# A two-block transformer in fp32: the order of the first projection after a stage boundary, and the place of one statistic on VectorE

## The reference

```python
def rms_norm(x, w):
    return x * rsqrt(mean(x * x, -1) + EPS) * w

def swiglu(h, w_in, w_out):                 # width 2816
    gate, up = split(h @ w_in, 2)
    return (silu(gate) * up) @ w_out

def memory_cross_attention(h, mem_n, w_q, w_k, w_v, w_o):   # 4 heads of 256
    q, k, v = h @ w_q, mem_n @ w_k, mem_n @ w_v
    return softmax(q @ k.T * 256 ** -0.5) @ v @ w_o

# first block
x = x + 0.5 * swiglu(rms_norm(x, ..), ..)
x = x + hybrid_mixer(rms_norm(x, ..), ..)   # a state-space scan beside differential attention
x = x + memory_cross_attention(rms_norm(x, ..), rms_norm(mem, ..), ..)
x = rms_norm(x + 0.5 * swiglu(rms_norm(x, ..), ..), ..)
# second block, two layers: ffn, mixer (pooling, then sparse attention), cross attention, ffn
for i in range(2):
    x = x + 0.5 * swiglu(..); x = x + mixer_i(..)
    x = x + memory_cross_attention_2(..); x = x + 0.5 * swiglu(..)
return rms_norm(x, final_norm)
```

## Time and profile before

| | |
|---|---|
| Time, median of 3 runs | 1930.49 us (1930.22 to 1930.87) |
| The profiled execution | 1930.22 us, its span 1928.4 us |
| TensorE busy | 1870.8 us, 97% of the span |
| VectorE busy | 1287.6 us, 67% |
| ScalarE busy | 972.1 us, 50% |
| GpSimd busy | 152.1 us, 8% |
| Mean granted TensorE clock | 0.989 of 2.4 GHz |
| DMA engines busy | 324.77 MB moved, mean 168 GB/s |

### The profile page before, as it was taken

The page is one execution under the profiler, slowest core; times in us unless marked ns, Lnnn a source line. Parts: engine busy times, 40 slices in busy tenths (PEclk is TensorE's granted clock), DMA queues, the critical chain, the costliest instruction groups (busy, mean ns, idle before and its releaser), DMA issues.

```text
span 1928.4 us, 32368 instructions
## 1 busy us (share of the span) xinstructions
PE 1870.8 (97%) x13202; PEld 1726.7 (90%) x13202; DVE 1287.6 (67%) x1454; ACT 972.1 (50%) x1322; POOL 152.1 (8%) x169
## 2 busy tenths in 40 slices
PE   6999999999999998999999999999999989999997
PEld 5999999899999997899999999989999859998997
DVE  5676687776566665766785766676668676456665
ACT  5454555575354444444554544454445564454444
POOL 2020100131010003000120100010001001010001
PEclk9999999999999998999999999999999989999998
DMA  6654454334445553554453455545545404435553
GB/s 237 223 197 174 153 186 154 143 123 163 155 150 189 182 188 142 193 187 183 153 197 132 161 189 176 194 175 184 187 176 189 165 23 153 155 125 202 188 182 109
DMA packets 45699, 324.77 MB, mean 168 GB/s; under 512 B 5165, under 2 KB 5301, under 8 KB 6688
## 3 DMA queue, kind: packets, MB, share of 16 engines
q1 hardware_dynamic: 44352, 316.57, 45.4%
q0 software_dynamic: 1248, 6.77, 1.0%
HBM read 322.26 MB, written 1.06 MB: 168 GB/s over the span
## 4 chain that ended last, share of the span: by engine, by line
PE 69%; DVE 7%; POOL 2%; ACT 1%; issue 1%; POOLq 0%; DVEq 0%; ACTq 0%
PE PS L638 20%; PE PS L545 11%; PE PS L546 11%; PE PS L547 11%; PE PS L641 10%; DVE w_lo L1968 3%; DVE xT L1991 2%; DVE x L2035 1%; PE PS L708 1%; PE PS L726 1%; POOL both L459 1%; PE PS L1219 1%; PE PS L1238 1%; PE PS L1258 1%; PE PS L579 0%
## 5 line engine op out<-in xcount | busy, mean ns | idle before, releaser
L1968 DVE TENSOR_TENSOR w_lo<-raw,w_hi 128x2048 fp32r<-128x2048 f32 x298 | 686.5, 2307 | 231.0 <-ACT w_hi L1307 230.7
L638 PE MATMUL PS<-xT,w_hi 128*128 128x512 f32 x2112 | 755.6, 401 | 17.0 <-DVE w_lo L1968 16.2
L1307 ACT ACTIVATE w_hi<-raw 128x2048 fp32r<-128x2048 f32 x299 | 571.1, 1911 | 306.9 <-PE PS L547 295.3
L641 PE MATMUL PS<-xT,w_lo 128*128 128x256 f32 x2112 | 595.0, 282 | 0.0
L638 PEld LDWEIGHTS PS<-xT,w_hi 128*128 128x128 f32 x2112 | 399.8, 189 | 113.6 <-issue 16.2
L641 PEld LDWEIGHTS PS<-xT,w_lo 128*128 128x128 f32 x2112 | 401.7, 190 | 0.2
L545 PE MATMUL PS<-h_hi,w_hi 128*128 128x256 f32 x1280 | 364.3, 285 | 0.0
L546 PE MATMUL PS<-h_lo,w_hi 128*128 128x256 f32 x1280 | 362.1, 283 | 0.0
L547 PE MATMUL PS<-h_hi,w_lo 128*128 128x256 f32 x1280 | 362.0, 283 | 0.0
L545 PEld LDWEIGHTS PS<-h_hi,w_hi 128*128 128x128 f32 x1280 | 245.1, 191 | 4.2 <-DVE h_lo L2115 1.0
L546 PEld LDWEIGHTS PS<-h_lo,w_hi 128*128 128x128 f32 x1280 | 245.2, 192 | 0.2
(11 more groups left out here) (310 smaller groups left out, 2492.4 us busy)
## 6 DMA issues: line engine op xcount, KB each, us to landing
raw<-weights SPq DMA_DIRECT2D x299, 1024.0 KB, 4.8
arena<-mems POOLq DMA_DIRECT2D x5, 1024.0 KB, 6.1
x<-x_in SPq DMA_DIRECT2D x2, 512.0 KB, 4.4
out<-x SPq DMA_DIRECT2D x4, 256.0 KB, 2.6
both<-toep POOLq DMA_DIRECT2D x1, 512.0 KB, 4.1
arena<-toep POOLq DMA_DIRECT2D x1, 512.0 KB, 5.4
con<-consts SPq DMA_DIRECT2D x1, 498.0 KB, 9.5
arena<-dtw SPq DMA_DIRECT2D x1, 256.0 KB, 11.3
```

The source lines that it names most:

```text
L638: pe.matmul(PS[:, bank + part, :], w_hi[:, slot, w:w + P], xT[:, k].rearrange("p a b -> p (a b)"), start=k == 0, stop=False, skip_group_ch ...
L641: last = pe.matmul(PS[:, bank + part, 0:S], w_lo[:, slot, w:w + P], xT_hi[:, k, :], start=False, stop=k == KC - 1, skip_group_check=True)
L1307: act.activation(w_hi[:, slot, :], raw[:, raw_slot, :], ACT.Copy).then_inc(hi_ready, 1)
L1968: dve.tensor_tensor(w_lo[:, slot, :], raw[:, raw_slot, :], w_hi[:, slot, :], ALU.subtract).then_inc(lo_ready, 1)
```

## The change

Two things are reordered; no operation is added or removed.

1. On TensorE, `proj` and `paired` run half 0 with all eight chunks and then half 1, also in the calls with `fresh`. Without `fresh` the order is what it was, and `mid` is still called after the first half. In a fresh call of `proj` the first step of half 1 now carries the flag `start`.
2. On VectorE, the cross stages make the eight low parts of the memory first and the statistic after them.

```diff
@@ proj
-                for part, first in ((0, 0), (0, 4), (1, 0), (1, 4)) if fresh is None else ((0, 0), (1, 0), (0, 4), (1, 4)):
-                    for k in range(first, first + 4):
+                for part in range(2):
+                    for k in range(KC):
                         if fresh is not None and part == 0:
                             pe.wait_ge(split_done, fresh * KC + k + 1)
...
-                        last = mm3(o, a, b, c, d, k == 0 and (part == 0 or fresh is None), k == KC - 1)
-                    if mid is not None and (part, first) == (0, 4):
+                        last = mm3(o, a, b, c, d, k == 0, k == KC - 1)
+                    if mid is not None and part == 0:
                         mid()
@@ cross, VectorE
-                statistic(rcol)
                 for c in range(KC):
                     low_part(c, memx, f"memn{at.mem}", mT_hi, mT_lo, mhi_ready, mlo_ready, at.mem)
+                statistic(rcol)
                 dve.wait_ge(rrow_ready, at.stat)
```

## The result

The changed kernel takes 1942.52 us, the median of 4 executions (1942.16 to 1943.93). The kernel before took 1930.36 beside it (4 executions, 1928.35 to 1930.87). The ratio is 1.0067, with a 95% interval of 1.0053 to 1.0082: slower by 0.67%, 12.2 us. I forecast 1942.0, in a range of 1937.0 to 1945.5. The total came out as forecast; not every term of it did, as will be seen.

The account below looks back on a forecast made before the run. TensorE, busy 1870.8 of 1928.4 us, was taken as the bound, with VectorE's diagonal deciding L579 in most stages. Statistic 6.3, order 2.4 and clock 3.0 gave 11.7 us more: 1942.0 us, range 1937.0 to 1945.5.

Parts of the forecast that it names:

- Part 1: Both cross stages: the statistic behind the memory's eight low parts delays the diagonal and L579 by 3.17 us each, 6.3 us.
- Part 2: First projection after stage boundaries: the new step order costs 2.4 us, mostly at FFN boundaries, after slack before L579.
- lateness d: How much later the first projection after a boundary ends in the new order: 1.06 to 1.42 us.
- the slack before L579 is 0.61: FFN at 560: printed idle 0.46 plus 0.15 absorbs part of 1.11 us lateness, leaving 0.50; two more boundaries repeat this.
- Cross clock: Both cross stages: TensorE stands still 2.57 us, then the clock falls to 1.2 GHz, 1.5 us each, 3.0 us.
- the 2.49 us before: Idle time at 1002.04: the clock fell to 0.50 soon after, and the projection took 7.32 us instead of 5.76.
- The clock did not hold: Rival for the cross stages: no clock fall, or one in two stages; 1939.2 to 1940.7 us, chance 0.29.
- The order in full: Rival at stage boundaries: slack before L579 absorbs no lateness, the new order costs 7.7 us; 1947.5 us, chance 0.12.
- The statistic was not hidden: Rival in the cross stages: sums come later than the low parts, making the move free; 1932.9 us, chance 0.06.
- faster: Rival at 749: TensorE works 1.4 us longer into its wait, keeping the clock up, about 1.5 us won; chance 0.02.

Follow-up runs that it names:

- two shifted kernels: The kernel before with 12 or 24 extra matmuls ahead of the NSA stage's third projection: 1933.09 us (1.0020) and 1934.69 us (1.0023).
- the statistic in the middle: The kernel before with four of the memory's eight low parts ahead of the cross stages' statistic and four behind, old step order: 1933.40 us, 1.0019.
- without the slack: The kernel before with the second weight split moved behind the diagonal: 1922.32 us in the old step order, 1934.41 us with the new order.
- two of the kernels here: Against the kernel before: second split behind the diagonal everywhere, 1922.32 us; the same except in FFN stages, where the row comes two steps later instead, 1926.24 us.

## Why the prediction was right, and where it was not

**Part 1, 6.3 us: right.** 3.16 us in each cross stage of the changed kernel, 3.19 and 3.16 with the statistic moved alone, half of it with half the move, 6.3 in the means (up to 7.2 when a quarter of the clock column is moved). All that was forecast of the place holds: ScalarE's high parts were no obstacle, nothing later in the stage gave the delay back, VectorE's evacuation was 1.21 us idle for ScalarE's row and nobody waited for it.

**Part 2, 2.4 us: right in kind, one term too large.** The first projection's lateness d was 1.07 in cross (forecast 1.06), 1.06 to 1.13 in the FFN (1.11), 1.36 at 1261 and 1.40 at NSA (1.42). It was absorbed as argued. But for each FFN boundary I put 0.50 where the changed kernel shows 0.12, 0.19 and −0.03, and 0.80 where it shows 0.61: 0.9 in place of 2.3. The step that failed is "the slack before L579 is 0.61", which takes the second projection's first half to be 16 uninterrupted matmuls and L579 to cost the same with or without a wait. Two rows show what it left out. The old second projection waited for its own weights; TensorE's weight loads of the kernel before, at 566:

```profile
566.02 0.19 PEld L638 LDWEIGHTS PS<-xT,w_hi 128*128 128x128 f32 x1 [0.17 <-DVE w_lo L1968]
```

and its matmul then, beside the same one after:

```profile
566.03 0.50 PE L638 MATMUL PS<-xT,w_hi 128*128 128x512 f32 x1
```

```profile
569.70 0.50 PE L571 MATMUL PS<-con,both 128*128 128x1 f32 x4
570.06 0.48 PE L638 MATMUL PS<-xT,w_hi 128*128 128x512 f32 x1
...
572.97 0.60 PE L579 MATMUL PS<-both,con 128*128 128x256 f32 x2
573.21 0.58 PE L638 MATMUL PS<-xT,w_hi 128*128 128x512 f32 x1
```

L638 follows L571 after 0.60 before (565.43 to 566.03) and after 0.36 now: 0.24 of lateness was there already, and the later projection hides it. And L579's row was 0.34 before its successor when it had waited (569.54 to 569.88) and 0.24 when it had not, 0.10 saved at each such boundary. 0.50 − 0.24 − 0.10 is 0.16, near the 0.12 to 0.19 measured. The −0.03 is counted well behind L579; directly behind it 0.09 is left. In the means over all executions the changed kernel has 1.7 us of waits beyond part 1, between the 0.9 and the forecast, and too coarse to choose.

**Cross clock, 3.0 us: right, with less certainty than one row can give.** 1.49 and 1.36 behind L579, after gaps of 2.61 and 2.62. The forecast rested on one row, the 2.49 us before; the same trace had two shorter gaps with a fall close behind, 1.94 at 25.64 (in the first stage, low from 26.75) and 1.89 at 1538.10 (low from 1538.85), and they were not used. Now six more stand beside it in front of L579: the clock fell after 2.61, 2.62, 3.48, 3.49 and 1.89, and did not after 1.91. But the pooling stage's gap itself, 2.46 to 2.50 us in all 12 traces, was passed without a fall in one of them (2.48, above), so a fall after 2.6 was likely and not certain. The Trainium skill ("TensorE: Matmul & The Clock Gate", section "Why this matters for your kernels") would have let all but the 3.48 and 3.49 pass; by that limit the falls after 2.49, 2.61, 2.62 and 1.89 should not be there, so the rows disagree with it, and bear out its advice to keep gaps short.

**What was not forecast: the clock elsewhere.** The profiled execution gained 1.5 in the first stage and 0.7 at 749 and lost 4.5 in the NSA stage. The means say 4.8 us of clock in all, or about 3.6 after the correction above, against 3.0 for the two falls I counted. So the total's distance of 0.5 us flatters the working, and it is partly luck. By the stages of the profiled execution the forecast terms came to 6.3, 0.9 and 2.9, 10.1 in place of 11.7, and 1.9 came from stages that no term names. The two shifted kernels lost such an amount of clock by a mere delay, but the kernel with the statistic in the middle, whose NSA stage starts 3.3 us later than before, did not (−0.3). Whether a delay costs clock on the whole was not found.

**The rivals.** The clock did not hold in either cross stage. The order in full is what happens without the slack (9.5), and only then. The statistic was not hidden: the sums were there at 456.4, a microsecond before the first memory low part began. The wait at 749 shrank from 8.03 to 6.62, and the longer projection in front of it did not keep the clock up: the granted clock was at the low level behind it both times. The 0.7 us that the stage gained are in good part clock all the same: the low stretch ended 6.67 us after L571 before (764.18 to 770.85) and 5.69 after it now (767.51 to 773.20), half of the difference being 0.5. With the statistic alone, where the projection is as before and the wait 8.03, that stage was shorter too (−0.9), so this is no gain by the mechanism of "faster".

## What to carry to other kernels

An instruction that is late on one engine is free for another up to the slack before the next shared wait, so the price of a reordering is read at that wait, not at the instructions moved; and the slack is what an uninterrupted run would leave, so look in it for smaller waits, which hide in the rows of weight loads. Where the last input of a short chain (sums, diagonal, row) has a queue of independent work in front of it on its engine, let the chain go first: here the one split that was put behind the statistic gave 7.9 us (some 5 of them waits, at L579 and, by way of GpSimd, at 749), and eight low parts in front of it cost 6.3 and the clock besides. Where a kernel's executions differ by microseconds, look at span and clock together, over several executions, before comparing edits of that size: two of the kernels here cannot be told apart by their waits and differ by 3.9 us in their times.

## What the runs showed of the hardware

- A gap of 1.89 us was followed by a granted clock of 0.50 and one of 1.91 was not, in one execution of one kernel; a gap of 2.48 us was passed at 1.00 in one trace, where gaps of 2.46 to 2.50 at the same place had a fall beside them in the other 11; the five falls behind L579 (two in the changed kernel, two with the statistic alone, one with it in the middle) cost 1.36 to 1.54 us each.
- 3.71 us of 32 matmuls of 128x32, without a gap, were followed by a fall to 0.50 in five of 12 traces and by none in seven.
- GpSimd's additions of 128x256 at 749 took 2.65 us when they started beside VectorE's weight split and 0.72 to 1.03 us otherwise.
- L579 takes 0.10 us more up to its successor when it had to wait for its semaphore than when it had not (0.34 against 0.24).
- The kernel before ran from 1927.14 to 1933.46 us in 27 executions on one chip, with clocks of 0.992 to 0.988. Span times clock ranged from 1907.0 to 1910.7 in them, the spans from 1925.3 to 1931.6.
- 24 extra matmuls, 2.88 us, made one profiled stage 5.1 us longer, 12 made it 0.77 longer; in the means the two kernels lost nearly the same clock, 1.4 and 1.2 us.
